# A conditioning projection moved from TensorE to GpSimd in a hybrid attention layer

## The reference, cut to what matters

```python
mod = jnp.einsum('bd,de->be', jax.nn.silu(c), w_ada) + b_ada            # w_ada: 1024 x 6144, one c for the prompt, one for the sample
sh1, sc1, gt1, sh2, sc2, gt2 = jnp.split(mod[:, None, :], 6, axis=-1)   # six conditioning vectors of 1024
h = rms_norm(x, g_norm1) * (1.0 + sc1) + sh1
q_a, k_a, v_a, q_idx, k_idx, w_idx, q_b, k_b, v_b, gate_a, gate_b = project_in(h, w_in)   # 4040 columns
y_a, y_b, state = mixer(...)      # A: top-256 of the keys by an indexer's score, then attention; B: windowed attention with sinks
merged = sigmoid(gate_a) * (y_a @ w_oa) + sigmoid(gate_b) * (y_b @ w_ob)
x = x + gt1 * (merged @ w_out)
h2 = rms_norm(x, g_norm2) * (1.0 + sc2) + sh2
x = x + gt2 * (relu(h2 @ w_up) ** 2 @ w_down)
```

## Time and profile before

| what | us |
|---|---|
| median of 3 runs (lowest, highest) | 1855.16 (1853.53, 1861.53) |
| the profiled execution, its time | 1853.04 |
| the profiled execution, its span | 1851.3 |
| PE busy | 1773.4 (96%) |
| DVE busy | 942.2 (51%) |
| ACT busy | 645.1 (35%) |
| POOL busy | 587.9 (32%) |

### The profile page before, as it was taken

One profiled execution on the slowest core, in us unless ns is written; L12 is line 12 of the kernel. 1 busy time (PEld: TensorE's weight loads), 2 busy tenths in 40 slices (PEclk: granted clock), 3 DMA queues, 4 the chain that ended last, 5 costly groups with the idle time before them and its releaser, 6 DMA issues.

```text
span 1851.3 us, 30123 instructions
## 1 busy us (share of the span) xinstructions
PE 1773.4 (96%) x11062; PEld 1688.0 (91%) x11062; DVE 942.2 (51%) x2290; ACT 645.1 (35%) x1253; POOL 587.9 (32%) x335
## 2 busy tenths in 40 slices
PE   7799999999989998999999999999999999999996
PEld 2688999999978887779999999999999999999996
DVE  1658888899256665555655542323323232323234
ACT  3545666641245555553322240303030303121212
POOL 0521222224667661112223222323222333223330
PEclk9899999999989998999999999999999999999998
DMA  7520224242342235653441111111111111111112
GB/s 273 166 46 24 71 87 111 94 132 82 121 121 71 72 88 134 175 150 113 136 166 57 34 46 46 46 44 36 45 45 45 45 37 43 45 45 45 45 34 97
DMA packets 179321, 153.47 MB, mean 83 GB/s; under 512 B 20240, under 2 KB 162016, under 8 KB 178688
## 3 DMA queue, kind: packets, MB, share of 16 engines
q1 hardware_dynamic: 175328, 137.31, 25.7%
q10 hardware_dynamic: 3920, 15.19, 2.0%
HBM read 127.34 MB, written 25.19 MB: 82 GB/s over the span
## 4 chain that ended last, share of the span: by engine, by line
PE 83%; DVE 6%; ACT 4%; DMA 3%; POOL 2%; issue 2%; SPq 0%; DVEq 0%; ACTq 0%; POOLq 0%
PE psum L887 66%; PE psum L1157 4%; PE psum L1184 2%; PE psum L1148 2%; PE psum L1011 2%; PE psum L1047 2%; PE psum L925 2%; POOL q_hl L807 1%; DVE h_f L1673 1%; DMA w_raw<-in_w_out 1%; DVE u_lo L2066 1%; PE psum L1127 1%; PE psum L1126 1%; DMA q_raw<-zT_scratch 1%; DMA out<-y_out 1%
## 5 line engine op out<-in xcount | busy, mean ns | idle before, releaser
L887 PE MATMUL psum<-h_hi,w_hi 128*128 128x362 f32 (+2 forms) x1440 | 474.6, 330 | 2.5 <-DVE h_lo L2044 1.6
L887 PE MATMUL psum<-h_lo,w_hi 128*128 128x362 f32 (+2 forms) x1440 | 474.1, 329 | 0.0
L887 PE MATMUL psum<-h_hi,w_lo 128*128 128x362 f32 (+2 forms) x1440 | 473.6, 329 | 0.0
L765 POOL CAST w_hi<-w_raw 128x1024 fp32r<-128x1024 f32 x112 | 125.0, 1116 | 1027.5 <-PEq L891 871.7
L767 POOL TENSOR_TENSOR w_lo<-w_raw,w_hi 128x1024 fp32r<-128x1024 f32 x112 | 281.6, 2515 | 9.0
L887 PEld LDWEIGHTS psum<-h_hi,w_hi 128*128 128x128 f32 x1440 | 271.2, 188 | 3.3 <-DVE h_lo L2044 1.9
L2028 DVE SCALAR_TENSOR_TENSOR xT<-psum,modT,xT 128x364 f32<-128x364 f32 (+3 forms) x288 | 136.1, 496 | 267.1 <-PE psum L887 267.1
L887 PEld LDWEIGHTS psum<-h_lo,w_hi 128*128 128x128 f32 x1440 | 271.5, 189 | 0.0
L887 PEld LDWEIGHTS psum<-h_hi,w_lo 128*128 128x128 f32 x1440 | 271.4, 188 | 0.0
L887 PE MATMUL psum<-u_hi,w_hi 128*128 128x362 f32 (+1 forms) x768 | 253.4, 330 | 3.2 <-DVE u_lo L2066 3.2
L1592 ACT ACTIVATE u_relu<-u_relu,b_up 128x364 f32<-128x364 f32 (+3 forms) x128 | 63.4, 519 | 553.5 <-DVE u_relu L2078 553.5
(11 more groups left out here) (289 smaller groups left out, 2885.1 us busy)
## 6 DMA issues: line engine op xcount, KB each, us to landing
w_raw<-in_w_in SPq DMA_DIRECT2D x32, 512.0 KB, 4.2
ada_c<-in_w_ada SPq DMA_DIRECT2D x32, 512.0 KB, 4.1
w_raw<-in_w_up SPq DMA_DIRECT2D x32, 512.0 KB, 4.1
w_raw<-in_w_down SPq DMA_DIRECT2D x32, 512.0 KB, 3.5
zT_scratch<-z_out ACTq DMA_DIRECT2D x27, 544.0 KB, 2.7
q_raw<-zT_scratch SPq DMA_DIRECT2D x32, 272.0 KB, 5.2
gate<-zT_scratch SPq DMA_DIRECT2D x16, 544.0 KB, 4.5
ada_w<-in_w_ada SPq DMA_DIRECT2D x4, 2048.0 KB, 8.8
```

Of the source, the lines that this page charges most:

```text
L765: pl.tensor_copy(w_hi[slot][:, :], w_raw[slot][:, :]).then_inc(sem("w_hi_made"), 1)
L887: ins = pe.matmul(bank(b, n), w[:, k, wc], x[:, a, c0:c0 + n], start=(m == 0 and p == 0), stop=(m == len(wk) - 1 and p == 2))
```

## The change

The four later vectors are made in two ways now.

- 24 of the 32 chunks (gt1, sh2, sc2; `NMAC = 24`) go to GpSimd. Behind the weight split of tile t of the projections, for t = 1 to 24, it accumulates one block of 128 rows by 1024 columns of `w_ada` (`accumulate`): for the prompt and for the sample a multiplication by the silu column and an addition, two of each (in the first block of each vector only the two multiplications). Each waits for its forerunner. SyncE loads the block (`load_mac`, 512 KB) between two loads of weights. TensorE adds over the partitions with `ones_col` (`add_parts`, 16 matmuls of one column), in tile 8, in tile 16 and behind tile 23; ScalarE copies the sums out.
- 8 chunks (gt2; `NADA = 8`) stay on TensorE in attention B, in every fourth unit.
- The scaling of the mask goes from GpSimd to ScalarE.
- The opening: the small vectors are loaded first, all nine token blocks have a slot of their own and are transposed and normalised beside the four `ada` blocks; ScalarE issues the stores of `xT`; both weight splits come ahead of the `h_lo` loop; the first two index tiles (`index_steps`) are multiplied between the last transposes and go through the groups side by side.
- The start of A: the first two masked biases are made ahead of the second query's split, in two further slots; that query is taken inside the last tile's evacuation, and one exponential ahead of the units. `cacheA` is loaded later, since `mac` has its place.

```diff
-        NADA = 4 * DM // P
+        NADA = DM // P
+        NMAC = 3 * KT
+        def mac_steps(q):
+            return 4 * q - 2 * -(-q // KT)
 # SyncE
+            def load_mac(q):
+                if q == 0:
+                    sp.wait_ge(sem("weighed"), NPIECE)
+                if q >= 2:
+                    sp.wait_ge(sem("mac_step"), mac_steps(q - 1))
+                sp.dma_start(w_mac[q % 2][:, :],
+                             bass.AP(w_ada.tensor, (q % KT) * P * 6 * DM + 2 * DM + (q // KT) * DM, [[6 * DM, P], [1, DM]]))\
+                    .then_inc(sem(f"mac_in{q % 2}"), 16)
...
+            load_x(0)
+            load_ada(0, 0)
+            for t in range(1, 5):
+                load_x(t)
+            load_ada(1, 1)
+            for t in range(5, NT):
+                load_x(t)
 # GpSimd
             split(0)
+            split(1, fresh=True)
...
-            splits(2, 2)
-            splits(3, 2)
-            splits(7, 2)
-            def scale_mask(c, name, rows_ready):
-                pl.wait_ge(sem("w_split"), 2 + jobs.n)
-                pl.wait_ge(sem("selected"), NSEL)
...
-                pl.tensor_scalar(selmask[:, c], selmask[:, c], -NEG_R, None, ALU.mult).then_inc(sem("mask_scaled"), 1)
...
+            def mac_step(ins):
+                ins.then_inc(sem("mac_step"), 1)
+                pl.wait_ge(sem("mac_step"), steps.next())
+            def accumulate(q):
+                k, part = q % KT, q // KT
+                pl.wait_ge(sem(f"mac_in{q % 2}"), 16 * (q // 2 + 1))
...
+                if k == 0 and part:
+                    pl.wait_ge(sem("sums_made"), part)
+                for s in range(2):
+                    silu = siluT[:, KT * s + k:KT * s + k + 1]
+                    if k == 0:
+                        mac_step(pl.tensor_scalar(mac[s][:, :], w_mac[q % 2][:, :], silu, None, ALU.mult))
+                    else:
+                        mac_step(pl.tensor_scalar(mac_term[:, :], w_mac[q % 2][:, :], silu, None, ALU.mult))
+                        mac_step(pl.tensor_tensor(mac[s][:, :], mac[s][:, :], mac_term[:, :], ALU.add))
+            for t in range(26):
+                split(t % 2)
+                if 0 < t <= NMAC:
+                    accumulate(t - 1)
...
             split_q(0)
+            bar_future(0, 0)
+            mask_bias(units[0])
+            mask_bias(units[1])
+            pl.wait_ge(sem("bias_masked"), made.n)
             split_q(1)
 # TensorE
+            def add_parts(part):
+                pe.wait_ge(sem("mac_step"), mac_steps(KT * (part + 1)))
...
+                for s in range(2):
+                    for c in range(KT):
+                        ins = pe.matmul(bank(7)[:, KT * s + c:KT * s + c + 1], mac[s][:, P * c:P * c + P], ones_col[:, 0:1],
+                                        start=True, stop=True)
+                ins.then_inc(sem("sums_made"), 1)
+            project(4)
+            project_tile(0, between=lambda g: add_parts(0) if g == 0 else None)
+            project_tile(1)
+            project(3)
+            project_tile(0, between=lambda g: add_parts(1) if g == 0 else None)
+            project_tile(1)
             project(2)
-            project(3)
-            project(6)
...
             project_tile(0)
             project_tile(1)
+            add_parts(2)
...
-                if 0 <= n - 1 - NA < NADA:
+                if n > NA and (n - 1 - NA) % 4 == 0 and (n - 1 - NA) // 4 < NADA:
                     pe.wait_ge(sem("y_done"), n - 2)
-                    ada_chunk(n - 1 - NA)
+                    ada_chunk((n - 1 - NA) // 4)
 # ScalarE
             ac.wait_ge(sem("selected"), NSEL)
             keys_hi(kA_hi[:, :], kA_raw[:, :], "kA_in", 32, "kA_hi_done")
+            ac.activation(selmask[:, 0:SEL_SAMPLE], selmask[:, 0:SEL_SAMPLE], ACT.Copy, scale=-NEG_R).then_inc(sem("mask_scaled"), 1)
+            gate_tile(13)
+            copy_sums(2)
```

More of the change, by code:

```diff
@@ L453, in steps_done @@
         def steps_done(pr, m):
-            first = 4 if pr == 0 else 0
+            first = KT if pr == 0 else 0
             return min(3 * KT, first + (3 * KT - first) * (m + 1) // PER_PAIR)
@@ L625, in load_bias_s @@
                       sem("biasS_in"))
[L627 to L630 removed]
+            project_beside(T_GATE, 5, 10)
             sp.wait_ge(sem("signs_counted"), SEL_BITS)
@@ L642, in _ @@
             load_bias_a(0)
-            project(T_GATE + 14, 1)
+            project_beside(T_GATE + 14, 1, 24)
             load_q(1)
+            sp.wait_ge(sem("sums_made"), 3)
+            for half in range(2):
+                sp.dma_start(cacheA[:, :, half, :], cache_k_a[0, 0].rearrange("(t p) d -> p t d", p=P))\
+                    .then_inc(sem("cacheA_in"), 16)
             for slot in range(2):
@@ L859, in _ @@
                     mask_sample(u["pair"], m - 4)
-                if u["blk"] is not None and u["blk"] >= 2:
+                if u["blk"] is not None and u["blk"] >= 2 and u["n"] >= 2:
                     mask_bias(u)
@@ L954, in _, with turn_normed @@
             turn_mod(0, 16, 1 + 4)
-            for t in range(NT):
+            def turn_normed(t):
                 n = P if t < NBLK else DEC
@@ L960, in _, with index_steps @@
                 for k in range(KT):
-                    ins = pe.transpose(bank(2 + 2 * (t % 2), 1024)[:, k * P:k * P + n],
-                                       x_tok[t % XRING][0:n, k * P:k * P + P], ident[0:n, 0:n])
+                    ins = pe.transpose(bank(2 + 2 * (t % 2), 1024)[:, k * P:k * P + n], x_tok[t][0:n, k * P:k * P + P],
+                                       ident[0:n, 0:n])
                 ins.then_inc(sem("xn_turned"), 1)
-                if t + AHEAD < NT:
-                    turn_x(t + AHEAD)
+            def index_steps(u, g, ks):
+                c0, n = GROUPS[g]
+                for k in ks:
+                    if k == 0:
+                        if g == 0:
+                            start_job()
+                        pe.wait_ge(sem("bank_free"), uses.next())
+                        pe.wait_ge(sem("h_lo_done"), -(-(c0 + n) // P))
+                    for p, (w, x) in enumerate(((w_hi, h_hi), (w_hi, h_lo), (w_lo, h_hi))):
+                        ins = pe.matmul(bank(IDX_BANKS[u, g], n), w[u][:, k * P:k * P + P], x[:, k, c0:c0 + n],
+                                        start=(k == 0 and p == 0), stop=(k == KT - 1 and p == 2))
+                    if k == 0 and (u, g) in ((0, 0), (1, 2)):
+                        pe.wait_ge(sem("acc_full"), uses.n)
+                        pe.sem_inc(sem("w_used"), 1)
+                if k == KT - 1:
+                    ins.then_inc(sem("acc_full"), 1)
+            for t in range(6):
+                turn_normed(t)
             pe.wait_ge(sem("xT_staged"), NT)
             pe.wait_ge(sem("mod_done"), 1)
+            index_steps(0, 0, range(4))
+            turn_normed(6)
+            index_steps(0, 0, range(4, KT))
+            turn_normed(7)
+            index_steps(1, 0, range(KT))
+            turn_normed(8)
+            for g in (1, 2):
+                for u in range(2):
+                    index_steps(u, g, range(KT))
             def turn_cache(m):
@@ L1019, in _ @@
             for step in range(4):
+                beside_step(0, step)
+            pe.wait_ge(sem("kIS_lo_done"), 1)
+            turn_cache(1)
+            for step in range(4, KT):
                 beside_step(0, step)
@@ L1251, in _ @@
                 turn_outputs(7, part)
-            for m in range(8):
+            for m in range(2):
                 ins = pe.transpose(bank(6, 1024)[:, m * P:m * P + P], ada_rows[:, m, :], ident[:, :])
@@ L1374, in _, with z_tile @@
             passes = Count()
-            def z_tile(u, before, dst, select=False):
+            def z_tile(u, before, dst, select=False, between=None):
                 ac.wait_ge(sem(f"z_stored{u}"), before)
@@ L1383, in z_tile @@
                         count_signs()
+                    if between and g == 1:
+                        between()
                 ac.wait_ge(sem("bank_free"), uses.n + NBANK)
```

257 lines of the change are left out of this document (140 added, 117 removed).

## The result

The changed kernel takes 1948.78 us (median of 4, 1944.31 to 1951.84), the kernel before 1856.19 (4 runs, 1853.53 to 1861.53): 1.0493 times as long, 95% interval 1.0472 to 1.0515. 1950 was forecast. The profiled execution has a span of 1944.1 us and took 1946.07. All runs count as fast but one of the eight of `e10_one_under_counts` (1871.80 us), which its ratio leaves out.

The account below looks back on a forecast made before the run. It took TensorE to bound the kernel, with VectorE an almost equal bound in the projections. Profiled 1853.0 + 141 (projections) − 45 (gains) = 1949; the median stands 2 us above that execution: 1950 us, range 1850 to 1985.

Parts of the forecast that it names:

- VectorE held by GpSimd's instructions: Projections: VectorE's short instructions wait for GpSimd's to end, 5.3 us a pass at full load; +120 us over 15 tiles.
- The ties: Projections, after the 32 passes: about 40 VectorE instructions may each wait for one of GpSimd's; +50 us, bounds 0 and 100.
- Behind `selected`: End of projections: only tile 25 and some transposes and copies, about 22 us, instead of 51 remain; −29 us.
- Gains: Attention B, opening and start of A together: −45 us.
- B: Attention B: 24 units without a chunk take 2.5 us each instead of 3.71; −29 us, bounds −15 and −44.
- The opening: Before the projections: last h_lo 4 us earlier, index tiles end about 94 instead of 107.85; −11 us, bounds −5 and −15.
- The start of A: Attention A's head: masks made before, leaving a bias, a maximum and an exponential; −5 us, bounds 0 and −7.
- VectorE is not held: First rival, projections: GpSimd is too slow but does not hold VectorE; +48 − 45, 1858 us; chance 0.13.
- the cast's price: Second rival, projections: multiplication costs the cast's 1.04 us and VectorE is not held; 1820 us, faster; chance 0.10.
- third rival: A rival given a chance of 0.10; the text given does not say clearly which claim it was.
- the clock: A case about the clock, partly outside the range; its wording is cut from the text given; chance 0.05.
- 1965: Attention B: time in us if the chunks gave nothing, since the queries' chain holds the units; inside the range.

Follow-up runs that it names:

- e10_one_under_counts: Changed kernel with one GpSimd multiplication a block, held by a wait until it lies under VectorE's counts; other multiplication and additions mostly left out: 1851.67 us, 0.9958.
- e7: Changed kernel with its GpSimd part undone: all 32 chunks on TensorE in attention B, new opening and head of attention A kept: 1851.65 us, 0.9963.
- e1: Changed kernel with 21 of 24 blocks' GpSimd multiplications and additions left out; loads, sums and the rest stay: 1851.94 us, 0.9974.
- e9: As e1, with 35 of the 48 sums over the partitions left out as well: 1839.54 us, 0.9902.
- e3: Changed kernel with a cast of the same 128x1024 in place of each GpSimd multiplication; the additions stay: 1941.31 us, 1.0439.
- e6: Changed kernel with only the prompt's multiplication and addition made on GpSimd, the sample's left out: 1904.09 us, 1.0262.
- e11: As e10_one_under_counts but without the wait, so the multiplication follows the split at once: 1875.05 us, 1.0097.
- e4: Changed kernel with six memsets of 128x1024 in place of each pair of multiplication and addition on GpSimd: 1935.43 us, 1.0417.
- e5: Changed kernel with each GpSimd multiplication and addition of a block made in four pieces of 256 columns: 1973.81 us, 1.0618.
- e8: As e7, with the third and fourth ada block loaded ahead of token blocks 5 to 8 and the first two weight tiles: 1842.56 us, 0.9917.

## Why the forecast was right, and where its steps were off

**VectorE held by GpSimd's instructions** was the deciding step, and it holds: as shown by place, by length and by kind. (The "L761" of the prediction is `cand`, L1761.) That a short instruction "ends when that one ends" holds beside the additions, the subtraction and the casts, beside the memsets for one tensor in, and not beside the multiplication, which held instructions with two tensors in only until 1.13 us of its 2.85, and those with one tensor in its first 1.1 and its last 0.9 us. The size was too large. I had three instructions, each waiting, 5.3 us at full load and 4.0 at 15 of 19.9 us; measured were five of them and 2.5 us in all. The formula took a mean of 2.56 us as the length of a hold, and the phase of GpSimd to be random, where it is locked to the pass; how much each of the two took off is not shown. Added up, 30 of the 83 us are behind the split. The passes lost 79 us, not 120.

**The ties** lost 23 us (89.3 instead of 66.4), not 50.

**Behind `selected`** I gave back 29 us, and 12 were lost: 62.8 instead of 50.8. This is the step with the wrong sign. I let tile 24 be ready, and did not follow SyncE past its wait for `selected`; and I put the sums at nothing. Two runs put 11 us to the load's order and 12 to the sums, over all three places of the sums. The three terms together were +141 and came to +114.

**Gains**, −45: B −13 instead of −29, as its chunk was hidden in part: 24 chunks of 1.84 us left, 44 us of TensorE, and 13 came back. The opening 0 instead of −11: the faster pace behind the modulation was there (43 us from it to the end of the first two index tiles instead of 55), but the modulation came 9 us late, behind four more token blocks on TensorE and its waits for loads and stores. I had bounded that at 5, and the 3 us that were left were lost by the end of the scores. The start of A −7 instead of −5.

So two errors of opposite sign, −27 in the projections and +25 in the gains, left the sum where it was, and the −27 is itself −41 in the passes, −27 in the ties and +41 behind `selected`. The mechanism was right; that the number came within 2 us is luck. The runs close the account another way: opening and head −5 (e7), B −13, sums +12 (e1 against e9, 35 of 48), arithmetic +97 (the changed kernel against e1; the 11 us of the load's order are in it), together +91 against 93 measured.

**The rivals.** That VectorE is not held falls with e3, e6, e10 and e11. The multiplication does not have the cast's price: 2.95 us against 1.10. The chances count a third rival at 0.10 and the clock at 0.05; no run shows a size for either, and what the runs showed in their place is this. With a cast where the multiplication was, VectorE is held as before: the passes end at 475.7 and the time is 1941.31 us (e3). The clock did fall, to 0.93 in the passes, where the holds alone account for the 79 us. Behind `selected` it cost some 5 us: it was 0.50 from 568 to 605, behind TensorE's rest, and the 32 instructions of the sums took 6.99 us and the 24 matmuls behind them 6.00, where the same took 3.65 us (e1, at 0.97) and 3.96 (the 24 behind those, at 1.00). One of the rivals' numbers does not come out as written: with nothing gained in B the sum is 1950 + 29 = 1979; 1965 is its bound of −15.

## What to carry to other kernels

An engine with a share of 32% has room only where its instructions may lie. Before work goes to GpSimd, look at what VectorE does in the same us: in these runs short instructions waited for the addition, cast or memset that they met (with two tensors in, not for a memset) and for parts of the multiplication (its first 1.1 of 2.85 us, and with one tensor in its last 0.9 too), VectorE's counts did not (876 ns on the mean, as before), and one semaphore wait that put the work under the latter took away all of its 28 us, where halving the work took away 23 of 78. Added work also moves what is there: splits that had cost nothing came to cost as much as the additions. When one engine's end moves, read the list of SyncE again: an order that was free while the others were late becomes the path.

## What the runs showed of the hardware

- GpSimd, 128x1024: a multiplication by a column 2.85 us, an addition 2.40 (the changed kernel), a copy 1.04 (e3), a memset 0.95 (e4); in pieces of 256 columns the multiplication 0.92 and the addition 0.74 us (e5; all medians).
- VectorE's one-input `TENSOR_SCALAR` of 1, 5 or 7 columns was held by GpSimd too, even by a memset (e4: means 622, 992 and 666 ns for `accept` of one and five columns and `flip`, against 143, 208 and 171 before); its `TENSOR_SCALAR_CACHE_REDUCE` of 384 to 896 columns had a mean of 876 or 877 ns in the passes of every kernel.
- GpSimd's multiplication by a column held VectorE in parts in the changed kernel: instructions with two tensors in until 1.13 us of its 2.85, those with one tensor in until 1.1 us and again from about 1.97 us to its end; from 1.17 to 1.73 us neither kind waited.
- Behind 32 matmuls of one column in a row, with no rest before, TensorE's clock fell from 1.00, three times of three in `e1_no_arith` (means of 0.50, 0.53 and 0.60 over the 4 to 7 us behind them); with 13 of the 48 sums (e9) or none (e7) it was 1.00 from 200 to 520.
- The runs of one kernel differ by 7 to 12 us (e8: 1841.09 to 1843.45 four times, 1849.29 and 1852.93; the kernel before beside e1: 1851.58 to 1863.37). The profiles show it in attention A. The same code there took from its first probabilities to B 185.6 us in e7 and 193.8 in e8, with these stretches of its middle, e7 first:

```profile
610.00:655.00 45.00, 42.64 (x338) 39.65 (x337) 31.19 (x97) 24.01 (x55) 30.84 (x21) 1.00 0.28 73
```

```profile
605.00:650.00 45.00, 42.83 (x323) 39.81 (x323) 29.47 (x95) 21.70 (x52) 30.48 (x20) 0.95 0.22 57
```

  The granted clock is lower and fewer instructions are done in the same time. Why it falls in one run and not in the next stays open.
